# A sparse expert layer: two whole-weight slots used in turn, in place of one slot with a prefetched half

## What is computed

```python
def moe_ffn(x, router_w, router_b, w1, b1, w2, b2):
    ...
    logits = (xf @ router_w + router_b).astype(jnp.float32)
    top_vals, top_idx = lax.top_k(logits, TOP_K)
    gates = jax.nn.softmax(top_vals, axis=-1)
    ...
    def expert_block(args):
        xblk, e = args
        h = xblk @ w1[e] + b1[e]
        g, u = jnp.split(h, 2, axis=-1)
        g = jnp.minimum(g, SWIGLU_LIMIT)
        u = jnp.clip(u, -SWIGLU_LIMIT, SWIGLU_LIMIT)
        act = g * jax.nn.sigmoid(SWIGLU_ALPHA * g) * (u + 1.0)
        return act @ w2[e] + b2[e]
    ...
```

## Time and profile before

| | us |
|---|---|
| median of 3 runs (lowest, highest) | 2908.08 (2902.8, 2915.6) |
| the profiled execution | 2914.63 |
| its span, first to last instruction | 2912.8 |
| first to last product of the expert stage in it | 1009.5 to 2881.5 |

### The profile page before, as it was taken

The page is one execution under the profiler, slowest core; times in us unless marked ns, Lnnn a source line. Parts: engine busy times, 40 slices in busy tenths (PEclk is TensorE's granted clock), DMA queues, the critical chain, the costliest instruction groups (busy, mean ns, idle before and its releaser), DMA issues.

```text
span 2912.8 us, 62643 instructions
## 1 busy us (share of the span) xinstructions
PE 2580.4 (89%) x22912; PEld 1102.3 (38%) x22913; DVE 1415.4 (49%) x2629; ACT 356.3 (12%) x910; POOL 646.9 (22%) x639
## 2 busy tenths in 40 slices
PE   8999999999989488799999989899899979997754
PEld 4644556544435223233333333233333323332212
DVE  4331456310143346466666656466556636664334
ACT  2000455300002100000000000000000000000002
POOL 0000000000001323234333323233333323332112
PEclk9999899999999699899999989999999989999877
DMA  4110000400054595911555465933885675569994
GB/s 137 58 43 0 8 8 1 152 22 29 0 183 123 154 352 201 353 24 24 196 195 195 147 242 193 364 100 120 315 300 199 249 262 180 195 240 387 388 376 137
DMA packets 166116, 499.13 MB, mean 171 GB/s; under 512 B 46273, under 2 KB 82497, under 8 KB 133057
## 3 DMA queue, kind: packets, MB, share of 16 engines
q1 hardware_dynamic: 108288, 459.90, 41.3%
q0 software_dynamic: 29168, 38.39, 7.2%
q10 hardware_dynamic: 28608, 0.19, 0.5%
HBM read 466.57 MB, written 32.15 MB: 171 GB/s over the span
## 4 chain that ended last, share of the span: by engine, by line
PE 45%; DMA 22%; issue 2%; DVE 1%; SPq 1%; DVEq 0%; ACT 0%; POOL 0%; ACTq 0%; POOLq 0%
PE xbank L1396 25%; PE xbank L1419 14%; DMA reg_r<-in_w 12%; DMA w_hi<-in_w 9%; PE xbank L1364 3%; PE xbank L1406 1%; PE xbank L1350 1%; PE xbank L1413 0%; SPq L991 0%; DVE reg_h L1326 0%; DMA stage<-xn_rows,idxg 0%; DMA w_hi<-in_b 0%; DVE reg_r L1296 0%; DMA reg_h<-acc_rows 0%; SPq L982 0%
## 5 line engine op out<-in xcount | busy, mean ns | idle before, releaser
L1296 DVE COPY reg_r<-reg_r 128x2048 f32 x580 | 680.3, 1228 | 395.4 <-issue 199.1
L1419 PE MATMUL xbank<-reg_r,stage 128*32 128x256 f32 x9280 | 561.5, 391 | 102.1 <-DMA reg_r<-in_w 102.1
L1396 PE MATMUL xbank<-reg_r,stage 128*32 128x512 f32 x4640 | 556.5, 617 | 104.3 <-DVE reg_r L1296 79.4
L1396 PE MATMUL xbank<-w_hi,stage 128*32 128x512 f32 x4640 | 584.8, 621 | 17.1 <-DMA w_hi<-in_w 17.0
L1419 PEld LDWEIGHTS xbank<-reg_r,stage 128*32 128x32 f32 x9280 | 287.3, 112 | 360.4 <-DMA reg_r<-in_w 130.7
L1396 PEld LDWEIGHTS xbank<-reg_r,stage 128*32 128x32 f32 x4640 | 146.7, 115 | 504.5 <-issue 396.4
L1044 POOL TENSOR_TENSOR idxs<-idxa,tok 128x1 int32<-128x1 int32 x145 | 44.0, 303 | 1039.0 <-ACT stage L1114 991.9
L1108 ACT ACTIVATE stage<-stage 128x256 f32<-128x256 f32 x145 | 60.5, 417 | 1746.2 <-DVE stage L1278 1746.2
L1047 POOL DMA_INDIRECT acc_rows<-stage,idxs x145 | 234.4, 1616 | 121.3 <-POOL idxs L1044 68.8
L1396 PEld LDWEIGHTS xbank<-w_hi,stage 128*32 128x32 f32 x4640 | 145.3, 113 | 290.4 <-issue 200.7
L1037 POOL DMA_INDIRECT stage<-xn_rows,idxg x147 | 226.7, 1542 | 120.9 <-POOL idxg L1034 112.4
(11 more groups left out here) (201 smaller groups left out, 2066.4 us busy)
## 6 DMA issues: line engine op xcount, KB each, us to landing
reg_r<-in_w SPq DMA_DIRECT2D x256, 1024.0 KB, 17.4
w_hi<-in_w SPq DMA_DIRECT2D x128, 1024.0 KB, 6.4
idxa<-slot_rows ACTq DMA_DIRECT2D x596, 0.2 KB
reg_r<-in_w_in SPq DMA_DIRECT2D x4, 2048.0 KB, 8.1
reg_g<-in_w_in SPq DMA_DIRECT2D x10, 512.0 KB, 3.8
reg_r<-in_x SPq DMA_DIRECT2D x8, 512.0 KB, 3.4
reg_r<-in_w_o SPq DMA_DIRECT2D x1, 4096.0 KB, 27.0
reg_h<-in_x SPq DMA_DIRECT2D x8, 512.0 KB, 7.7
```

Source lines behind the costliest of these rows:

```text
L1296: dve.tensor_copy(w1k[k], lo_from[:, bass.ds(slot, 1), k, :].rearrange("p o n -> p (o n)")).then_inc(w1_filled[k], 1)
L1396: ins = pe.matmul(up_bank[b][QB * c:QB * c + QB, :].rearrange("p (h k q) -> p h k q", h=2, q=QB), xT[b][:, QB * k:QB * k + QB], w1k[k].rea ...
L1419: ins = pe.matmul(y_bank[b][QB * j:QB * j + QB, 0:DG], actT[b][:, QB * k:QB * k + QB], w2r[:, k, j * DG:(j + 1) * DG], start=False, stop=( ...
```

## The change

The on-chip memory of both halves becomes one tensor `big` of six regions of 4 MiB. In the expert stage regions 0 to 2 are weight slot 0 and regions 3 to 5 are slot 1, each with room for a whole expert. Even blocks use slot 0, odd blocks slot 1. The experts are sorted on chip by their number of blocks (expert 0 stays first, expert 31 last); even blocks take blocks from the front of that list, odd blocks from its back. So slot 0 sees experts of 1, 18, 9, 9, 9, 8, 8, 7 and 7 blocks, of the last one 3, and slot 1 sees 4, then 1 four times, 2 eight times, 3 four times, 4, 5, 5, 6, 6, 6 and the other 4 blocks of the expert in the middle. That one is loaded into both slots: there are 33 loads of an expert in place of 32. A list `events` of 31 entries (after how many blocks, which expert, which slot) drives SP: eight `w1` pieces and then four `w2` pieces for each entry. The copies on DVE, `next_lo` and `w1_filled` are gone.

The rest goes with it. The first pieces of expert 31 are loaded ahead of the stage, `w1` 4 to 7 of it only when the list is ready, since the routing's work tiles lie in region 5. The routing loop is two turns shorter, with `logits` between the two halves of the output product. The list takes more steps. ACT fetches a block's indices in one DMA with a source that is read four times. The descriptor space of POOL's DMAs is halved, from the default to 8192.

```diff
-        w1_half = [reg_r[:, 0:8192].rearrange("p (k n) -> p k n", k=4), w1_hi[:, :].rearrange("p (k n) -> p k n", k=4)]
-        w1k = [w1_half[k // 4][:, k % 4, :] for k in range(KD)]
-        w2r = reg_r[:, 8192:16384].rearrange("p (k n) -> p k n", k=KD)
-        next_lo = reg_r[:, 16384:].rearrange("p (k n) -> p k n", k=4)
-        lo_from = reg_r[:, :].rearrange("p (s k n) -> p s k n", s=3, k=4)
-        w2q = [w2r[:, 2 * q:2 * q + 2, :] for q in range(W2P)]
-        stage = sb("stage", [P, 6 * D])
...
+        slots = big[:, :].rearrange("p (s r k n) -> p s r k n", s=2, r=3, k=4)
+        w1k = [[slots[:, b, 0 if k < 4 else 2, k % 4, :] for k in range(KD)] for b in range(2)]
+        w2q = [[slots[:, b, 1, q, :].rearrange("p (k n) -> p k n", k=2) for q in range(4)] for b in range(2)]
+        w2r = [region(big, 3 * b + 1).rearrange("p (k n) -> p k n", k=KD) for b in range(2)]
+        stage, routing = region(big, 5)[:, 0:6 * D], region(big, 5)[:, 6 * D:]
...
             for q in range(W2P):
-                sp.dma_start(w2q[q], w2_d[0, q]).then_inc(w2_in[q], 16)
+                sp.dma_start(w2q[0][q], w2_d[0, q]).then_inc(w2_in[q], 16)
+
+            def load_last(k):
+                sp.wait_ge(w1_in[k], 16)
+                sp.dma_start(w1k[1][k], w1_d[NEXP - 1, k]).then_inc(w1_in[k], 16)
             for k in range(4):
-                sp.wait_ge(w1_in[k], 16)
-                sp.dma_start(next_lo[:, k, :], w1_d[1, k]).then_inc(w1_in[k], 16)
+                load_last(k)
+
+            sp.wait_ge(acc_out, 16 * NT)
+            sp.wait_ge(rms2_ready, NT)
+            sp.wait_ge(xn_ready, NT)
+            for q in range(W2P):
+                sp.wait_ge(w2_in[q], 16)
+                sp.dma_start(w2q[1][q], w2_d[NEXP - 1, q]).then_inc(w2_in[q], 16)
+
+            sp.wait_ge(tab_out, 16 * NT * TOPK)
+            for n in range(2):
...
+                freed = sp.value_load(events[0:1, 0, bass.ds(j, 1)], min_val=1, max_val=NBLOCKS + 1)
+                e = sp.value_load(events[0:1, 1, bass.ds(j, 1)], min_val=0, max_val=NEXP - 1)
+                slot = sp.value_load(events[0:1, 2, bass.ds(j, 1)], min_val=0, max_val=1)
...
+                    sp.wait_ge(w1_used[k], freed)
+                    sp.wait_ge(w1_in[k], j * 16 + 32)
+                    sp.dma_start(slots[:, bass.ds(slot, 1), 0 if k < 4 else 2, k % 4, :].rearrange("p o n -> p (o n)"),
+                                 w1_d[bass.ds(e, 1), k].rearrange("o p n -> (o p) n")).then_inc(w1_in[k], 16)
                 for q in range(W2P):
-                    sp.wait_ge(w2_used[q], ended)
-                    sp.dma_start(w2q[q], w2_d[bass.ds(i + 1, 1), q].rearrange("o p k n -> (o p) k n")).then_inc(w2_in[q], 16)
-
-            def load_next_lo(i, ended, k):
-                sp.wait_ge(w1_filled[k], ended)
-                sp.dma_start(next_lo[:, k, :], w1_d[bass.ds(i + 2, 1), k].rearrange("o p n -> (o p) n")).then_inc(w1_in[k], 16)
-            with sp.Fori(0, NEXP - 2) as i:
-                ended = sp.value_load(listi[0:1, 2, bass.ds(i, 1)], min_val=1, max_val=NBLOCKS)
-                load_hi(i, ended)
-                load_next_lo(i, ended, 0)
...
-            ended = sp.value_load(listi[0:1, 2, NEXP - 2:NEXP - 1], min_val=1, max_val=NBLOCKS)
-            for k in range(4, KD):
-                sp.wait_ge(w1_used[k], ended)
-                sp.dma_start(w1k[k], w1_d[NEXP - 1, k]).then_inc(w1_in[k], 16)
...
-                sp.dma_start(w2q[q], w2_d[NEXP - 1, q]).then_inc(w2_in[q], 16)
+                    sp.wait_ge(w2_used[q], freed)
...
+                if t >= 2:
+                    act.wait_ge(top_ready, t - 1)
+                    act.activation(ex[:, t - 2, :], top[:, t - 2, 0:TOPK], ACT.Exp, bias=ntop[:, t - 2:t - 1],
+                                   accum_out=exs[:, t - 2:t - 1]).then_inc(ex_ready, 1)
...
+                    act.wait_ge(idx_in[b], half * 16)
                 row = act.value_load(listi[0:1, 1, bass.ds(n, 1)], min_val=0, max_val=TABROWS - QB)
-                for j in range(NG):
-                    act.dma_start(idxa[QB * j:QB * j + QB, bass.ds(n, 1), :].rearrange("p o v -> p (o v)"),
-                                  tab_d[bass.ds(row, QB), :]).then_inc(idx_in[b], 16)
+                act.dma_start(idxa[:, bass.ds(n, 1), :].rearrange("p o v -> p (o v)"),
+                              tab_d[bass.ds(row, QB), :].unsqueeze(0).to_broadcast([NG, QB, 2])).then_inc(idx_in[b], 16)
 
             def sigmoid(n):
...
-            for t in range(NT + 4):
+            for t in range(NT + 2):
                 if 1 <= t <= NT:
                     norm(t - 1)
-                if 2 <= t <= NT + 1:
-                    store_xn(t - 2)
-                if 3 <= t <= NT + 2:
-                    best(t - 3)
-                if t >= 4:
-                    place(t - 4)
                 if t < NT:
-                    residual(t)
+                    residual(t, 0)
+                if t >= 2:
+                    best(t - 2)
+                if t < NT:
+                    residual(t, 1)
+                if 1 <= t <= NT:
...
+            dve.tensor_copy(part_e[:, :], part_c)
+            dve.drain()
+            dve.tensor_scalar(over, iota_32e[0:32, :], count, None, ALU.is_lt)
+            dve.drain()
+            dve.tensor_reduce(nb, over, AX.X, ALU.add)
+            dve.drain()
+            dve.tensor_scalar(nb, nb, 1.0, None, ALU.max)
+            dve.drain()
+            dve.scalar_tensor_tensor(out=key, in0=nb, scalar=key_mul, in1=key_add, op0=ALU.mult, op1=ALU.add)
+            dve.drain()
+            dve.tensor_scalar(diag_k, ident[0:32, 0:32], key, None, ALU.mult).then_inc(key_ready, 1)
+            dve.wait_ge(key_done, 1)
+            dve.tensor_scalar(more, bank[3][0:32, 0:32], key, None, ALU.is_gt)
+            dve.drain()
...
-            def refill(n):
-
-                loaded = dve.value_load(listi[0:1, 0, bass.ds(n, 1)], min_val=16, max_val=16 * NEXP)
-                slot = dve.value_load(listi[0:1, 3, bass.ds(n, 1)], min_val=0, max_val=2)
-                for k in range(4):
-                    dve.wait_ge(w1_used[k], n)
-                    dve.wait_ge(w1_in[k], loaded)
-                    dve.sem_inc(refill_go, 1)
-                    dve.tensor_copy(w1k[k], lo_from[:, bass.ds(slot, 1), k, :].rearrange("p o n -> p (o n)")).then_inc(w1_filled[k], 1)
+                dve.tensor_tensor(gl, ul, sg, ALU.mult)
+                dve.drain()
+                dve.transpose(actT[b], gl).then_inc(act_ready, 1)
 
...
             turn_x(1, 1, 0)
             n_iters = block_iters(dve)
-            refill(1)
             swiglu(0, 0)
             turn_x(2, 0, 1)
             with dve.Fori(0, PAIRS) as i:
                 with dve.If(i < n_iters):
                     for m in range(2):
                         n = i * 2 + (m + 1)
...
+            for t in range(NT + 2):
                 if t < NT:
-                    out_product(t)
+                    out_product(t, 0)
+                if t >= 2:
+                    logits(t - 2)
+                if t < NT:
+                    out_product(t, 1)
                 if 1 <= t <= NT:
                     turn_xn(t - 1)
-                if 2 <= t <= NT + 1:
-                    logits(t - 2)
-                if t >= 3:
-                    rank(t - 3)
+                if t >= 2:
+                    rank(t - 2)
...
-                    if k < 4 and not isinstance(n, int):
-                        pe.wait_ge(w1_filled[k], n)
-                    else:
-                        pe.wait_ge(w1_in[k], loaded)
+                    pe.wait_ge(w1_in[k], loaded)
                     for c in range(NG):
...
                     for m in range(2):
                         n, b = i * 2 + (m + 1), 1 - m
+                        now = weights_of(n)
                         pe.wait_ge(xT_ready, n + 1)
                         pe.wait_ge(up_taken, n)
-                        up(n, b, None, range(0, 4))
-                        now = weights_of(n)
+                        up(n, b, now, range(0, 4))
                         up_bias(n, b)
-                        up(n, b, now, range(4, 6))
+                        up(n, b, now, range(4, 7))
...
 
-    nc = bacc.Bacc("TRN2", target_bir_lowering=False, num_devices=1)
+    nc = bacc.Bacc("TRN2", target_bir_lowering=False, num_devices=1, dynamic_dma_scratch_size=8192)
```

More of the change, by code:

```diff
@@ L791, in expert_constants @@
     p = np.arange(P)
[L792 removed]
+    f = np.zeros((P, 480), np.float32)
     f[:, 0:32] = np.arange(32)[None, :]
@@ new lines, in expert_half @@
+        row_of = rt(NEXP)
+        maskb = rt(NT * NEXP // 2).bitcast(BF16).rearrange("p (t e) -> p t e", t=NT)
+        l32 = lists[0:32, :]
+        past, turn_q, hot_p = l32[:, 0:NPAD], l32[:, 168:168 + NPAD], l32[:, 336:336 + NPAD]
+        over, diag_k, diag_t, more, perm, event_of = (l32[:, 512 + 32 * n:544 + 32 * n] for n in range(6))
+        step_e = l32[:, 704:800]
+        l_cols = l32[:, 800:864]
```

(7 more changed lines are left out.)

327 lines of the change are left out of this document (192 added, 135 removed).

## The result

The changed kernel takes 2829.35 us (median of four runs, 2824.4 to 2834.2) against 2908.97 us (with a fourth run of the kernel before, 2909.86): a ratio of 0.972, 95% interval 0.969 to 0.975. The forecast was 2826, in a range of 2765 to 2885. The sum came out within 4 us. Its parts did not all do so: one mechanism that moves 30 to 40 us was missing, and two of the priced terms had another cause than the one named. That the errors cancelled is luck.

The account below looks back on a forecast made before the run. How fast weights come decides: 327 of the stage's 1872 us were lost. New stage 1545 + 240 of waits + 10 for the fetch = 1795, 77 less; start 5 earlier; median 2826 us, range 2765 to 2885.

Parts of the forecast that it names:

- The price of a block: Expert stage on PE: one block takes 10.65 us without a gap, and new register reads add nothing.
- The floor: Expert stage if PE never waited: 7.1 + 144 x 10.65 + 3.6 = 1545 us.
- One-block experts: Slot 1's four one-block experts: 12 MiB wanted every two blocks, 34.2 us against 21.3, 52 us in all.
- Six meetings: Both slots switch on neighbouring blocks six times, queueing 24 MiB: 24 us each, 144 us in all.
- The start of the stage's loads: Block 2 waits for weights, as four pieces for slot 1 are issued only when the list is ready: 20 us.
- Single switches: The other 20 switches, where the last `w2` piece arrives with nothing to spare: 20 us, 0 to 50.
- the first meeting's 4 us: A switch after block 39, following the first meeting, finds the load queue still full: 4 us.
- the second rival: Meetings and short experts cost as much as the old switches: single switches 3.5, meetings 27, 2880 to 2922 us; chance 12%.
- Index fetch: ACT's fetch as one transfer loads one DMA engine and delays the weight stream: 10 us more, 0 to 28.
- The start, 5 us earlier: Ahead of the stage: routing ends two turns sooner, stage starts 12 us earlier to 20 later, 5 earlier taken.
- Loads all hidden: Rival: with two whole slots PE never waits for weights in the expert stage, 2576 us; chance 2%.
- The stream is slowed: Rival: slower weight stream and kernel, at the last quarter of `w2` in a single switch, margin 0 to 1 us; chance 8%.

Follow-up runs that it names:

- e3: The changed kernel without the 31 expert loads of the expert stage, SP only raising the counts: 2594.96 us in one run.
- e2: The changed kernel with one expert of seven blocks moved from eighth to third place in the sorted list: 2763.15 us.
- e6: The changed kernel with four index fetches of 32 rows and the seven-block expert third in the list: 2706.81 us.
- e11: The changed kernel with four index fetches, a fixed block order worked out for this routing, and bias rows chosen before turning gathered rows: 2646.76 us.
- e9: The changed kernel with DVE choosing the next block's bias rows before turning the gathered rows, not after: 2799.87 us.
- e5: The changed kernel with its one index fetch of 128 rows issued two blocks earlier: 2805.80 us.
- e1: The changed kernel with its index fetch as before, four transfers of 32 rows instead of one of 128: 2788.72 us.
- e10: The changed kernel with both bias rows chosen before turning gathered rows and four index fetches of 32 rows: 2769.32 us.
- e4: The kernel before with its four index fetches a block made one transfer of 128 rows: 2893.23 us, ratio 0.9955.

## Why the prediction held, step by step

- **The price of a block, 10.65 us: right.** It is the median distance of two blocks, 10.65 or 10.66 us, in every run, so the new register reads cost nothing, though one takes PE's sequencer 0.30 us in the trace and the loop's branch 0.22 (where the text took 0.2).
- **The floor, 1545: 11 us low.** Two terms failed: "the last `down` stands alone (3.6)" takes 11.7, and the first block 9.6 and not 7.1 (e3). Both were in the 1872 of before as well (11.3 and 8.9), so 327 us lost should have read 317.
- **One-block experts, 52: 45 measured.** The mechanism is right; the pairs last 32 to 33 us and not 34.2.
- **Six meetings, 24 each, 144: 130 measured**, 20.7 to 22.4 each, all on the blocks that were named. The 13th queued piece came 39 us after the first was issued (1455.2 to 1494.3), 3.0 us a piece, within the 2.85 to 3.05 used. e2 shows the cause: 66 us for one expert's place in the list. The edit takes four meetings away, and with four fetches (e6) each is worth 21 us of stage.
- **The start of the stage's loads, 20: 10 measured** (block 2).
- **Single switches, 20 us, "limited by the 4th `w2` piece": the step that failed.** Together with the first meeting's 4 us and the 10 for the fetch the forecast had 34, and 43 were measured, but not there. The text set as its own mark that no wait in `up` should show in a single switch. 13 of 14 show one, for the bias rows, and `down` waits nowhere. The count was off too: of the prediction's own 31 switches 12 are in meetings, 4 follow a one-block expert and one follows block 0, which leaves 14 and not 20 with 4 more. At 40 us in sum each cost near 3 us, over the 2.5 of the upper end and near the 3.5 of the second rival. The one after block 39, priced at 4 us, cost nothing (block 41 takes 10.7). In e11 single switches cost 0: the last `w2` piece is in time, as forecast. Its margin is as thin as computed, though: in e9, with PE a little ahead and weights a little later, three of them do wait for it, 1.5 us at most.
- **Index fetch, 10 (0 to 28): the right size for the wrong half.** What was priced, a delay of the weight stream, fits the 10 us that e5 leaves against e1, and up to 21 in e9 against e10 (which holds whatever else separates the two). The upper 28 was the author's estimate, and no run shows the delay of a block that it needs. Not priced was that the fetch would be late: 18.5 us of stage (e5) and the start. The prediction had POOL and the bias rows in view ("for which I count nothing"), and the list of before held a wait for `sel`, 16.8 us in 14 places, that was passed over. The whole form costs 28.5 us of stage, 41 of the median; that the 28.5 met the upper 28 is luck, as most of it is lateness. The form shows in the packets of q10: 19668 are 149 fetches of 132, 128 rows and 4 completions, where four fetches of 32 rows have 28608 = 149 x 192, 128 rows and 64 completions.
- **The start, 5 us earlier: 0.3 measured.** The list was ready in time: its chain on DVE took 11.7 us (974.1 to 985.8) where it took 6.2 before (981.2 to 987.3), 5.5 more. The first index fetch went out at 989.6, 12 us earlier. But POOL had its index only 12.1 us after that and not 3.2, beside the queued weight pieces, and the gather behind it took 3 us longer too (5.9 for 2.9). The versions with one fetch start at 1004 to 1011, those with four at 997 to 1007. With "twelve pieces queued may hold the scatters' landing" the text had the cause, on the wrong transfer. No run shows the terms behind the range's 20 us later: a slot scatter takes POOL 0.97 us in both kernels, and the first index fetch follows the last scatter by 11.5 us (978.1 to 989.6), where it was 13.0 (988.8 to 1001.8).
- **The rivals.** "Loads all hidden" was off by 253 us. "The stream is slowed" didn't come: 3.0 us a piece in the first meeting, under the mark of 3.2, and `down` waits at no piece of `w2` in the changed kernel.

So the mechanism of meetings and one-block experts held, and the total was right within 4 us because errors cancelled, which is luck. In the stage: meetings and one-block experts 21 us less than forecast, the start's loads 10 less, the floor 10 more (here the last `down` takes 11.6 us and the first block 8.7), single switches and fetch 9 more, in sum 12 under the 1795. The start came 5 later than taken. The profiled run was thus 2824.4 and not 2832.6, and its median lies 5 above it, where the prediction took it 6.5 below.

## What to carry to other kernels

When each of two slots is refilled while the other works, count on which blocks the refills fall: two that fall together cost here 21 us each time, and moving a single expert in the list took four of six away. A small transfer that another engine's program waits for has to be priced by when it lands beside the full stream (here 10 to 19 us after its issue, and 2.6 without the stream), not by its bytes; look at the slack between its issue and its use, and at what stands behind the waiting instruction on each engine, down to an operation of 0.2 us. And before trusting a sum, ask of every wait in the list of before, the small ones too, what makes it longer when the engine it belongs to runs faster.

## What the runs showed of the hardware

- A fetch of 128 rows of 8 bytes as one transfer, with 4 completions: 2.6 us when quiet, 10 to 19 beside a weight stream (349 GB/s from 1357 to 1376, 394 to 416 in the meeting shown). As four transfers of 32 rows: 2.7 and 5.5 to 9.9. The share of the queue is 0.4 and 0.5% in the two forms, so the share told nothing of it. A fetch behind another on the queue moved nothing until that one had ended (1375.20 after 1375.19, and 0.0 to 0.8 us after it in the 49 places of the changed kernel where it was issued over 0.5 us before).
- With the same form the old kernel took 0.45% less (e4), which is near what can be told; the cause is open.
- PE's clock: a wait of 2.92 us (block 45) was followed by a granted 1.00 over 10 us and cost 3.1 us. One of 3.76 (block 29) was followed by a granted 0.81 and cost 5.5, one of 3.99 (block 33) by 0.73 over 11 us and cost 7.1. One of 3.15, in a meeting (block 91), was followed by 0.67 over 5 us. The meeting shown falls to 0.56 for 10 us (1495 to 1505).
